# HGRN block: projection pieces spread over the level steps, cross products ahead of the mixed values

## The reference

```python
proj = h @ w_in                                  # 1024 -> q, fl, v, g, 1024 each
q = silu(q);  k = (1 - lb) * sigmoid(-fl)
log_f = log(lb + (1 - lb) * sigmoid(fl))         # per token, head and feature
S_t = diag(f_t) S_{t-1} + k_t v_t^T              # a state of 128 x 128 for each head
o_t = S_t^T q_t
o = o * rsqrt(mean(o * o) + EPS) * norm_w        # over the 128 values of a head
out = (o.reshape(B, S, 1024) * silu(g)) @ w_out
```

## Time and profile before

| | |
|---|---|
| median of 3 runs | 1012.35 us (1012.14 to 1012.42) |
| profiled execution | 1012.22 us |
| its span | 1010.4 us |
| TensorE busy | 981.1 us, 97% of the span |
| VectorE, ScalarE, GpSimd busy | 71%, 47%, 8% |

### The profile page before, as it was taken

The page is one execution under the profiler, slowest core; times in us unless marked ns, Lnnn a source line. Parts: engine busy times, 40 slices in busy tenths (PEclk is TensorE's granted clock), DMA queues, the critical chain, the costliest instruction groups (busy, mean ns, idle before and its releaser), DMA issues.

```text
span 1010.4 us, 13344 instructions
## 1 busy us (share of the span) xinstructions
PE 981.1 (97%) x5460; PEld 853.2 (84%) x5460; DVE 712.8 (71%) x744; ACT 475.2 (47%) x543; POOL 81.8 (8%) x74
## 2 busy tenths in 40 slices
PE   7999999999999999999889999999989999999997
PEld 7888888878888887998878888888879888888886
DVE  5565766877776676668757866667779978666674
ACT  4576546544443354532124544443358845434341
POOL 0400000000000001007520000000012100000000
PEclk9999999999999999999999999999999999999999
DMA  7755334654645553653203765555335637555631
GB/s 259 260 188 203 125 126 137 218 186 153 236 175 210 207 208 117 236 190 106 104 8 118 265 214 185 190 198 178 125 126 188 215 145 282 175 203 175 207 120 42
DMA packets 27133, 176.89 MB, mean 175 GB/s; under 512 B 3392, under 2 KB 3648, under 8 KB 7488
## 3 DMA queue, kind: packets, MB, share of 16 engines
q1 hardware_dynamic: 26784, 174.98, 48.9%
q10 hardware_dynamic: 288, 1.05, 0.3%
HBM read 174.97 MB, written 1.05 MB: 174 GB/s over the span
## 4 chain that ended last, share of the span: by engine, by line
PE 41%; DVE 6%; issue 2%; ACT 1%; DMA 0%; POOL 0%; POOLq 0%; DVEq 0%; ACTq 0%; SPq 0%
PE ps L1590 15%; PE ps L1593 8%; PE ps L1563 6%; PE ps L1564 6%; PE ps L1565 6%; DVE wL L954 2%; PE ps L1942 1%; PE ps L1609 1%; DVE FF L1470 1%; DVE FF L1494 1%; DVE RR L966 0%; DMA raw<-w_stream 0%; DVE FF L1490 0%; ACT wH L528 0%; DVE FF L1483 0%
## 5 line engine op out<-in xcount | busy, mean ns | idle before, releaser
L954 DVE TENSOR_TENSOR wL<-raw,wH 128x2048 fp32r<-128x2048 f32 (+2 forms) x158 | 355.8, 2262 | 97.6 <-ACT wH L528 97.6
L528 ACT ACTIVATE wH<-raw 128x2048 fp32r<-128x2048 f32 (+2 forms) x158 | 292.5, 1859 | 117.0 <-PE ps L1593 54.8
L1590 PE MATMUL ps<-aHL,wH 128*128 128x512 f32 x864 | 215.8, 392 | 0.0
L1590 PEld LDWEIGHTS ps<-aHL,wH 128*128 128x128 f32 x864 | 157.2, 189 | 29.4
L1563 PE MATMUL ps<-wL,RR 128*128 128x512 f32 (+1 forms) x384 | 150.2, 391 | 0.4 <-DVE RR L966 0.3
L1564 PE MATMUL ps<-wH,RR 128*128 128x512 f32 (+1 forms) x384 | 149.2, 388 | 0.0
L1565 PE MATMUL ps<-wH,RR 128*128 128x512 f32 (+1 forms) x384 | 148.9, 388 | 0.0
L1563 PE MATMUL ps<-wL,aHL 128*128 128x512 f32 (+2 forms) x304 | 122.6, 403 | 4.9 <-ACT aHL L539 3.3
L1593 PEld LDWEIGHTS ps<-aHL,wL 128*128 128x128 f32 x864 | 117.9, 190 | 8.4
L1593 PE MATMUL ps<-aHL,wL 128*128 128x256 f32 x864 | 120.5, 282 | 0.0
L1565 PE MATMUL ps<-wH,aHL 128*128 128x512 f32 (+2 forms) x304 | 117.1, 385 | 0.0
(11 more groups left out here) (225 smaller groups left out, 1130.7 us busy)
## 6 DMA issues: line engine op xcount, KB each, us to landing
raw<-w_stream SPq DMA_DIRECT2D x152, 1024.0 KB, 4.8
raw<-w_stream SPq DMA_DIRECT2D x6, 512.0 KB, 3.6
FF<-rows_in SPq DMA_DIRECT2D x5, 512.0 KB, 7.1
raw<-w_stream SPq DMA_DIRECT2D x4, 576.0 KB, 4.8
bc<-rows_in SPq DMA_DIRECT2D x4, 512.0 KB, 7.8
raw<-w_stream SPq DMA_DIRECT2D x2, 768.0 KB, 9.0
xn<-rows_in SPq DMA_DIRECT2D x1, 1024.0 KB, 4.2
out<-xn SPq DMA_DIRECT2D x4, 256.0 KB, 2.3
```

Of the source, the lines that this page charges most:

```text
L528: e.activation(weight_slot(i)[0][:, 0:wd], raw[:, i % NRAW, 0:wd], ACT.Copy).then_inc(hi, 1)
L954: e.tensor_tensor(l[:, 0:wd], raw[:, i % NRAW, 0:wd], h[:, 0:wd].bitcast(F32), ALU.subtract).then_inc(lo, 1)
L1590: e.matmul(ps[:, b, :], h[:, cs[k]], aHL[:, k].rearrange("p i t -> p (i t)"), start=k == 0, stop=False)
```

## The change

The 12 pieces are placed otherwise: behind steps 0, 1, 2, 3, 5, 7, 9, 11, 13 and 15, then one behind both mixed values and one behind the turning of tile 0. The pieces of the last gate columns are ordered by token tile instead of by chunk, and that of tile 1 gets a bank of its own. The products across blocks come before `mix_v(0)`. TensorE's step no longer waits for GpSimd's combined decays, only for `K`. VectorE does `grow` and `gather` first and makes low halves and gates behind them, at other steps; chunk 80's halves and the last gates move behind the first tile's heads. ScalarE's list follows. The number of matmuls, copies and transfers is the same.

```diff
@@ ScalarE: copies, sigmoids and splits
-            for n in range(1, 4):
-                ...
-                split(ck[1] + 4)
-                ...
+            split(77)
+            v_in(0)
+            v_in(1)
+            split(79)
+            g_in(2, 0)
+            g_in(2, 1)
+            split(80)
+            g_in(3, 0)
             for g in range(2):
                 e.wait_ge(cross, g + 1)
...
             head_square(0)
-            from_flip(("heads", 0, 0), act, 4, 4)
-            from_flip(("heads", 0, 1), act, 5, 4)
             head_square(1)
+            from_flip(("heads", 0, 0), act, HEADS_BANK[0][0], 4)
+            from_flip(("heads", 0, 1), act, HEADS_BANK[0][1], 4)
+            split(81)
+            g_in(3, 1)
             split(82)
@@ VectorE
-            SPLITS = {2: 77, 4: 78, 6: 79, 8: 80, 10: 81}
-            G_AT = {6: (2, 0), 7: (2, 1), 10: (3, 0)}
+            SPLITS = {3: 77, 5: 78, 9: 79, 13: 80}
+            G_AT = {11: (2, 0)}
             for step in range(16):
-                lev, g = step // 2, step % 2
+                grow(step % 2, step // 2)
+                gather(step % 2, step // 2)
                 if step in SPLITS:
                     split(SPLITS[step])
                 if step in G_AT:
                     g_rows(*G_AT[step])
-                grow(g, lev)
-                gather(g, lev)
-            g_rows(3, 1)
+            g_rows(2, 1)
+            g_rows(3, 0)
...
-                if t == 0:
-                    e.wait_ge(g_mul, 8)
+                if t == 1:
+                    g_rows(3, 1)
+                e.wait_ge(g_mul, 6 + 2 * t)
...
+            heads_sum(0)
             heads(0)
-            from_flip(("heads", 0, 0), act, 4, 4)
-            from_flip(("heads", 0, 1), act, 5, 4)
+            heads_sum(1)
+            from_flip(("heads", 0, 0), act, HEADS_BANK[0][0], 4)
+            from_flip(("heads", 0, 1), act, HEADS_BANK[0][1], 4)
+            split(81)
             heads(1)
@@ TensorE
                     if lev > 1:
-                        e.wait_ge(hg_k, 4 * (lev - 2) + 2 * g + 2)
+                        e.wait_ge(hg_k, 4 * (lev - 2) + 2 * g + 1)
...
+            PIECES = {step: f for f, step in enumerate((0, 1, 2, 3, 5, 7, 9, 11, 13, 15))}
             for step in range(16):
                 level(step % 2, step // 2)
-                if step < 11:
-                    hg_piece(step)
-            hg_piece(11)
+                if step in PIECES:
+                    hg_piece(PIECES[step])
...
+            for g in range(2):
+                b0 = 4 + 2 * g
+                e.wait_ge(hg_q, 15 + g)
+                e.wait_ge(hg_k, 25 + g)
+                e.wait_ge(gathered, 15 + g)
+                ...
+                last.then_inc(cross, 1)
...
             mix_v(0)
-            for g in range(2):
-                ...
-                last.then_inc(cross, 1)
             mix_v(1)
...
+            hg_piece(10)
             flip_heads(0)
+            hg_piece(11)
             e.wait_ge(head_mul, 1)
             project("hgrn_w_out", "heads", lambda: flip_heads(1))
```

More of the change, by code:

```diff
@@ L781, in _, with v_in, g_in, head_square @@
             split(76)
-            for n in range(1, 4):
-                b = 2 if n % 2 else 0
-                ck = a_at("hgrn_w_in", 2048 + 512 * n, 512, 8)
-                split(ck[1] + 4)
-                for t in range(2):
-                    if t == 0:
[L788 to L799, removed]
+            def v_in(t):
+                if t == 0:
+                    e.wait_ge(half, HALF["hg", 1])
+                else:
+                    e.wait_ge(used, a_at("hgrn_w_in", 2560, 512, 8)[1] + 1)
+                copy(V[:, t, 512:1024], HG_BANK[1][t], 512)
+            def g_in(n, t):
+                if t == 0:
+                    e.wait_ge(half, HALF["hg", n])
+                else:
+                    e.wait_ge(used, a_at("hgrn_w_in", 2048 + 512 * n, 512, 8)[1] + 1)
+                e.activation(G[:, t, 512 * n - 1024:512 * n - 512], ps[:, HG_BANK[n][t], :], ACT.Sigmoid).then_inc(g_sig, 1)
+            def head_square(t):
+                e.wait_ge(head_out, 2 * t + 2)
+                e.activation(xn[:, t, :].rearrange("p (b n) -> p b n", b=2), ps[:, 2 * t:2 * t + 2, :], ACT.Square
+                             ).then_inc(head_sq, 1)
+            split(77)
[6 more added lines that the diff above has]
+            g_in(3, 0)
             for g in range(2):
@@ L1953, in hg_piece @@
                         e.wait_ge(squared, SQUARE["post_mlp", 1, 1])
-                    else:
-                        e.wait_ge(copied, COPY["hg1", t])
-                last = a_part(held(i) if t else weights(i), 512, act, t, 4 * c, 0, 4, 8, b + t)
+                    elif t == 0:
+                        e.wait_ge(copied, COPY["hg1", 0])
+                    else:
+                        e.wait_ge(gathered, 15)
+                last = a_part(held(i) if t else weights(i), 512, act, t, 4 * c, 0, 4, 8, HG_BANK[n][t])
                 if t:
@@ L1960, in hg_piece @@
                     last.then_inc(half, 1)
+            PIECES = {step: f for f, step in enumerate((0, 1, 2, 3, 5, 7, 9, 11, 13, 15))}
             for step in range(16):
                 level(step % 2, step // 2)
-                if step < 11:
-                    hg_piece(step)
-            hg_piece(11)
+                if step in PIECES:
[5 more added lines that the diff above has]
+                e.wait_ge(gathered, 15 + g)
+                for h in range(4):
+                    last = e.matmul(ps[:, b0, 128 * h:128 * h + 128], K[:, 4 * g + h, 0:128],
+                                    Q[:, 4 * g + h, 128:256], start=True, stop=True)
+                last.then_inc(cross, 1)
             def mix_v(t):
                 for g in range(2):
-                    if t:
-                        e.wait_ge(cross_in, 2)
[L1972 to L1977, removed]
+                    if t == 0:
+                        e.wait_ge(g_mul, 2 * g + 1)
+                        if g == 0:
+                            e.wait_ge(copied, COPY["hg1", 1])
+                    elif g == 0:
+                        e.wait_ge(cross_in, 2)
+                        e.wait_ge(g_mul, 5)
                     for h in range(4 * g, 4 * g + 4):
```

31 lines of the change are left out of this document (16 added, 15 removed).

## The result

The changed kernel takes 1006.0 us (median of 4 runs, 1005.62 to 1006.4), the kernel before 1012.38 us in the same comparison (1012.14 to 1015.8). The ratio is 0.9922, with a 95% interval of 0.9908 to 0.9937. The two medians by themselves stand at 0.9937; one of the four runs of the kernel before took 1015.8. The forecast was 1007.0 in a range of 1006.0 to 1009.3: the direction and the place of the gain were right, but more was won than the sum gave. The profiled execution took 1005.83 us, its span 1003.9 instead of 1010.4.

A forecast was written before the change was run, and what follows sets the result against it. TensorE was taken to bound the kernel, with only its HGRN idle time to win: 5.7 us if nothing waits, less 0.4 of stalls, gives 5.3; 1012.35 - 5.3 = 1007.0 us, range 1006.0 to 1009.3.

The forecast's parts named there:

- the five waits: TensorE idle ahead of step 12, `mix_v(1)`, turning, output projection and inside the turning (2.53, 0.69, 1.08, 0.97, 0.39 us): all go.
- step with piece: HGRN part, TensorE: a level step followed by one projection piece takes 4.55 us.
- products plus `mix_v(0)`: HGRN part behind the steps, TensorE: products across blocks and first mixed values together take 3.56 us.
- turning: HGRN tail, TensorE: turning the heads of tile 0 takes 0.8 us start to start.
- piece: HGRN part, TensorE: one projection piece takes 2.85 us.
- The halves of chunk 81: Output projection: VectorE's low half ends just ahead of part four, with 0.6 us of slack.
- a step followed by a step takes 1.93: HGRN level steps, TensorE: a step directly behind another costs 1.93 us, so a pair with one piece lasts 6.48 us.
- The 0.4 us of stalls at the steps: HGRN level steps: VectorE's queue makes steps late, 0 to 0.9 us at step 8; 0.4 us put down for all.
- the first wait: TensorE's 2.53 us ahead of step 12: put down to step 10's `grow` standing behind a late low half on VectorE.
- B: HGRN level steps: VectorE and GpSimd exclude each other's SBUF operations and bound the steps, 2.4 us lost, 1009.0 us; 16%.
- C: HGRN tail and later: small slacks fail and idle time only moves, 1011.0 us, no measurable change; 5%.
- D: HGRN level steps: every VectorE operation, gathers too, excludes GpSimd's, making the kernel slower, 1018.4 us; 5%.

The follow-up runs named there:

- `before_filled_free`: Kernel before, its four HGRN idle places filled with unused identity matmuls and TensorE's steps waiting only for GpSimd's K: 1013.3 us, ratio 0.9995.
- `before_fill_tail`: Kernel before, unused identity matmuls ahead of `mix_v(1)`, the turning and the output projection, none ahead of step 12: 1012.83 us, ratio 0.9997.
- Three filled kernels: Kernel before with unused identity matmuls in its four HGRN idle places, measured twice (1013.52, 1013.4 us), and once with steps waiting only for K (1013.3 us).
- the second comparison: Changed kernel, unaltered, measured again against the kernel before: 1005.24 us against 1013.68, ratio 0.9921.
- `after_wait_decays`: Changed kernel, but TensorE's steps wait for GpSimd's combined decays again: 1007.24 us, ratio 0.9938.

## Why the prediction was right in its mechanism, and which step failed

**Right.** That TensorE's idle time was the whole prize and that each of the five waits would go: the bracketless rows above. Each cover was large enough: products ahead of `mix_v(0)` (0.69 us back when undone), pieces 10 and 11 (3.8 us of waits when undone). Of the terms, step with piece (4.55, measured (457.85 - 444.25) / 3 = 4.53), products plus `mix_v(0)` (3.56, measured 3.57), turning (0.8, measured 0.79) and piece (2.85, measured 2.85 and 2.82) held. The halves of chunk 81 came in time, as worked out (low half ends 522.29, part four starts at 522.83).

**The step that failed: the term "a step followed by a step takes 1.93" was mis-sized.** I took 1.70 from the 7.51 us of steps 12 to 15 and divided the rest by three, and so took for work what held a wait inside. A step costs 1.78; a pair (468.72 - 462.39) 6.33 and not 6.48. Six pairs make 0.9 us. The wait stood at step 14: 0.29 us on the weight loads, whose releaser the profile gives only as "issue", in this row of the kernel before:

```profile
503.00 3.65 PEld L1942 LDWEIGHTS ps<-FF 128*128 128x128 f32 x32 [0.29 <-issue]
```

By `before_filled_free` it is GpSimd's, part decays, part K. `mix_v(1)` takes 3.49 and not 3.67 partly for a like reason: 0.1 us was its first matmul's start behind a wait, the other 0.1 comes from what follows, as a piece starts 0.14 us behind the last mixed value and not 0.22.

**The 0.4 us of stalls at the steps didn't come.** With the shorter pairs no step is late. The operations that VectorE took beside GpSimd were about as long as I took them (2.87, 1.10, 1.04 us), but only some of them. These are the 1.6 us by which 6.90 exceeds the 5.3 of the sum: 0.9 + 0.2 + 0.4, and 0.1 of small differences. The brackets of the earlier trace rows add up to 5.27 us; the other 1.6 that were won stood in rows that show no bracket.

**The named cause of the first wait was wrong.** "Step 12 waits for step 10, whose `grow` stands behind a low half that starts late" is true of the order and false of the cause: without the low half the wait is the same 2.53 us, without the gates it is 0.18. The prediction had the `g_rows` in the queue too, but not what it waits for. The sum was not hurt, since the change moves both.

**A term was missing: the granted clock.** The table groups the 29 runs of the kernel before by mean granted clock.

| mean granted clock | runs | time |
|---|---|---|
| 0.996 to 0.997 | 10 | 1012.07 to 1012.87 us |
| 0.995 | 6 | 1013.02 to 1014.18 us |
| 0.993 | 7 | 1014.3 to 1015.82 us |
| 0.990 to 0.992 | 6 | 1016.61 to 1017.18 us |

One stretch of 3.4 us at half clock is 0.0017 of the mean, and costs 1.36 us where it falls on dense work: steps 12 to 15 take 7.75 us in the kernel before and this in `before_fill_tail`:

```profile
498.89 9.11 PE L1946 MATMUL ps<-FF 128*128 128x128 f32 x64 [2.53 <-DVE FF L1367]
```

 Three filled kernels gave 31 runs with none at 0.993 or under; the kernel before gave 22 of 54 beside them. The median of 1012.35 that I started from was of three runs (1012.14 to 1012.42) that by their times belong to the first group, without such extra stretches. Among 17 profiles, 9 had an idle time of TensorE of 1.08 us or more in the HGRN part, and 5 of these a dip behind one; of the other 8 (at most 0.72 us at once) none had a dip. The changed kernel belongs to the 8. Its LRU still dips now and then behind its wait, as in the first profile after (749.4 to 752.8). That accounts for the 0.64 us given back: up to the LRU's wait the two profiles after agree within 0.05 us, and the second, without that dip, has a span of 1003.1. Between profiles without dips the change is worth 1010.4 - 1003.1 = 7.3 us; between the means of the second comparison, 1013.73 - 1005.48 = 8.2. The runs of that comparison with a mean clock of 0.996 or more say the same as the profiles: 1012.19 and 1012.3 before, 1004.9 to 1005.43 after, 7.1 us. That the difference of about 1 us is the dips is likely and not shown, because filling the waits did not bring it: the filled kernels' fastest runs are some 0.5 us slower than the kernel before's. That loss doesn't lie in the HGRN part: from step 12 to the turning `before_filled_free` takes 518.68 - 499.15 = 19.53 us, the kernel before 19.70. Part of it lies behind: in the three profiles with all four places filled, one matmul at 569 to 571 us starts 0.28 to 0.45 us behind the one ahead of it, in the two of the kernel before 0.12. Why stays open.

**The rivals.** B (VectorE and GpSimd bound the steps) has its mechanism on the chip and not its effect: GpSimd's decays are held for a low half, but VectorE's steps fit and TensorE doesn't wait for the decays, which B had counted into a pair's 8.4 us. Even with the old wait, in `after_wait_decays`, 0.7 and 0.3 us appear and not B's 2.4. C fell: no slack failed. D fell: `grow` and `gather` of a pair end in time throughout.

## What to carry to other kernels

A duration taken as the mean of a run of like instructions must be checked for waits inside; a loader's idle time with the releaser "issue" is one. Before a wait is put down to the slowest instruction ahead of the late one, ask of each instruction ahead what *it* waits for: here a short gate product, waiting for a sigmoid, cost more than the 3 us subtraction. And where TensorE idles, half-clock time may follow and belongs into the range: moving real work into the gap took such stretches away as well, filling it with useless matmuls did not pay.

## What the hardware showed unexpectedly

- The granted clock fell to 0.50 (1.2 GHz) for 3.4 us around idle times of TensorE of 0.97 to 2.53 us, in some executions and not in others of the same program. The 17 profiles have 13 such stretches between 30 and 1000 us, six in the HGRN part and seven in the LRU; each begins between 0.6 us ahead of the end of such an idle time and 1.5 us behind it. Idle times of 1.58 us at 54 us and 1.32 us at 82 us are in every profile, and none is followed by a stretch. The Trainium skill, "TensorE: Matmul & The Clock Gate", Part 1, says that activity holds the full clock and that idle time gives it up; the places of the dips agree, the fall after waits as short as these was new to me.
- A GpSimd operation with SBUF operands that becomes due while VectorE's subtraction of two SBUF inputs runs is held until that is done, whatever its own size: 0.21 us alone, 2.26 beside it. That is the rule of the Trainium skill, "SBUF — State Buffer", section "Who interferes with whom"; the prediction gave it 16% for the effect, and the trace agrees with the rule. By the rule alone the result would have been rival B's 1009.0; it held and the time was another, because TensorE no longer waited for what was held. A gather, which reads PSUM, leaves GpSimd alone: a product took 1.32 us beside one and 1.31 without.
